# Gated-delta inverse: the last level computed as one 64-row quarter

## The reference, cut to what matters

```
kk = jnp.einsum('bhnid,bhnjd->bhnij', k, k)
lower = jnp.where(strict, beta[..., :, None] * kk * decay, 0.0)
rhs = jnp.concatenate([v * beta[..., None], k * (beta * jnp.exp(g_cum))[..., None]], axis=-1)
sol = lax.linalg.triangular_solve(lower + eye, rhs, left_side=True, lower=True, unit_diagonal=True)
```

## Time and profile before

| | us |
|---|---|
| median of three runs | 3823.49 |
| lowest, highest | 3817.28, 3826.62 |
| the profiled execution | 3812.9 |
| its span, first to last instruction | 3811.1 |
| granted TensorE clock, mean over the span | 0.97 |
| TensorE matmuls busy | 3521.2 (92%) |
| VectorE busy | 2263.3 (59%) |
| ScalarE busy | 1843.9 (48%) |
| subtractions of the inverse, line 1868 | 60.4 (88 instructions) |

### The profile page before, as it was taken

The page is one execution under the profiler, slowest core; times in us unless marked ns, Lnnn a source line. Parts: engine busy times, 40 slices in busy tenths (PEclk is TensorE's granted clock), DMA queues, the critical chain, the costliest instruction groups (busy, mean ns, idle before and its releaser), DMA issues. The chain is left out here.

```text
span 3811.1 us, 44895 instructions
## 1 busy us (share of the span) xinstructions
PE 3521.2 (92%) x18342; PEld 2970.9 (78%) x18342; DVE 2263.3 (59%) x2508; ACT 1843.9 (48%) x2354; POOL 610.4 (16%) x208
## 2 busy tenths in 40 slices
PE   7989899999899996899999899899998799999999
PEld 6879777788788875688888778787888468787887
DVE  4566569675666667666667555545455555545654
ACT  4454356664456552456554344444443344444443
POOL 0001149571133320142401100000000000000000
PEclk9999999999999998999999999999999899999999
DMA  5532156565376752376742145454544125454453
GB/s 221 188 133 89 45 210 248 216 250 189 116 270 236 265 199 100 145 265 241 263 160 96 57 147 188 163 188 155 188 168 160 38 89 188 158 191 148 155 204 133
DMA packets 89977, 653.55 MB, mean 171 GB/s; under 512 B 10033, under 2 KB 10033, under 8 KB 10929
## 3 DMA queue, kind: packets, MB, share of 16 engines
q1 hardware_dynamic: 78768, 573.10, 41.5%
q0 software_dynamic: 11008, 77.60, 5.7%
HBM read 649.61 MB, written 1.05 MB: 171 GB/s over the span
## 5 line engine op out<-in xcount | busy, mean ns | idle before, releaser
L1562 DVE TENSOR_TENSOR w_lo<-raw,w_hi 128x2048 fp32r<-128x2048 f32 x540 | 1420.9, 2636 | 646.7 <-ACT w_hi L1080 646.4
L1080 ACT ACTIVATE w_hi<-raw 128x2048 fp32r<-128x2048 f32 x540 | 1031.2, 1913 | 592.2 <-PE acc L521 403.3
L519 PE MATMUL wrk<-w_hi,h_hi 128*128 128x512 f32 (+1 forms) x2496 | 971.2, 389 | 58.8 <-DVE w_lo L1562 37.9
L521 PE MATMUL wrk<-w_hi,h_lo 128*128 128x512 f32 (+1 forms) x2496 | 954.7, 382 | 0.0
L520 PE MATMUL wrk<-w_lo,h_hi 128*128 128x512 f32 (+1 forms) x2496 | 953.9, 382 | 0.0
L519 PEld LDWEIGHTS wrk<-w_hi,h_hi 128*128 128x128 f32 x2496 | 472.5, 189 | 155.2 <-DVE w_lo L1562 48.9
L2308 POOL TENSOR_TENSOR arena<-arena,c 128x2048 f32<-128x2048 f32 x92 | 490.7, 5342 | 472.6 <-ACT arena L1080 447.6
L521 PEld LDWEIGHTS wrk<-w_hi,h_lo 128*128 128x128 f32 x2496 | 472.2, 189 | 92.5
L520 PEld LDWEIGHTS wrk<-w_lo,h_hi 128*128 128x128 f32 x2496 | 472.8, 189 | 85.0 <-issue 0.2
L519 PE MATMUL acc<-w_hi,hid_hi 128*128 128x512 f32 x1144 | 447.4, 391 | 9.4 <-DVE hid_lo L1645 9.4
L521 PE MATMUL acc<-w_hi,hid_lo 128*128 128x512 f32 x1144 | 445.4, 389 | 0.0
(11 more groups left out here) (263 smaller groups left out, 3864.5 us busy)
## 6 DMA issues: line engine op xcount, KB each, us to landing
raw<-in_wts SPq DMA_DIRECT2D x540, 1024.0 KB, 4.8
arena<-in_mods POOLq DMA_DIRECT2D x72, 1024.0 KB, 5.2
const<-in_const SPq DMA_DIRECT2D x1, 2176.0 KB, 10.1
c<-in_bias POOLq DMA_DIRECT2D x8, 256.0 KB, 3.4
x<-in_x SPq DMA_DIRECT2D x1, 1024.0 KB, 5.3
c<-in_c SPq DMA_DIRECT2D x1, 1024.0 KB, 4.8
out<-x SPq DMA_DIRECT2D x1, 1024.0 KB, 3.9
row<-in_rows SPq DMA_DIRECT2D x1, 512.0 KB, 11.3
```

The lines of the kernel that those rows point to most:

```text
L519: nc.tensor.matmul(o, l_h, r_h, start=first, stop=False, skip_group_check=True)
L521: return nc.tensor.matmul(o, l_l, r_h, start=False, stop=last, skip_group_check=True)
L1080: return nc.scalar.activation(o, i, f, **kw)
L1562: tt(w_lo[:, ns % SLOTS, :], raw[:, ns % SLOTS, :], w_hi[:, ns % SLOTS, :].bitcast(F32), ALU.subtract).then_inc(lo_ready, 1)
```

## The change

At the last level the two blocks to be joined are the rows 0 to 63 and 64 to 127. The masked matrix has entries only in rows 0 to 63 and columns 64 to 127. The changed kernel multiplies at that level only 64 rows by 64 columns with 64 moving columns for X and YT, puts the four results side by side in 256 columns of 64 partitions of the bank, copies only that quarter and subtracts only that quarter from `g_u`. X lies on partitions 64 to 127, YT on partitions 0 to 63. Levels 0 to 4, all waits and the order of instructions are as before.

```diff
 # TensorE, X
-                                m = mm(o[:, b * P:(b + 1) * P], g_lts[:, lv % 2, 4 * a + b, :], g_vi[:, 4 * a + b, :], start=True, stop=True)
+                                if lv < nl - 1:
+                                    m = mm(o[:, b * P:(b + 1) * P], g_lts[:, lv % 2, 4 * a + b, :], g_vi[:, 4 * a + b, :], start=True, stop=True)
+                                else:
+                                    m = mm(o[64:P, b * 64:(b + 1) * 64], g_lts[0:64, lv % 2, 4 * a + b, 64:P], g_vi[0:64, 4 * a + b, 0:64], start=True, stop=True)
...
 # TensorE, YT
+                                        if lv < nl - 1:
+                                            m = mm(o[:, b * P:(b + 1) * P], lh[:, 4 * a + b, :], rh[:, 4 * a + b, :], start=True, stop=True)
+                                        else:
+                                            m = mm(o[0:64, b * 64:(b + 1) * 64], lh[64:P, 4 * a + b, 0:64], rh[64:P, 4 * a + b, 64:P], start=True, stop=True)
...
 # ScalarE
+                            if lv < len(LEVELS) - 1:
+                                copy_out(f"X{half}{lv}{grp}", g_xs[:, 4 * a:4 * a + 4, :])
+                            else:
+                                label = f"X{half}{lv}{grp}"
+                                full(label)
+                                frees(use[name, label])
+                                fn(g_xs[64:P, 4 * a:4 * a + 4, 0:64], bk(label)[64:P, 0:256].rearrange("p (a b) -> p a b", b=64), ACT.Copy).then_inc(taken, 1)
...
 # VectorE
-                                    v = flat(t[:, 4 * a:4 * a + 4, :])
-                                    tt(v, v, bk(l_), ALU.subtract).then_inc(taken, 1)
+                                    if lv < len(LEVELS) - 1:
+                                        v = flat(t[:, 4 * a:4 * a + 4, :])
+                                        tt(v, v, bk(l_), ALU.subtract).then_inc(taken, 1)
+                                    else:
+                                        v = t[0:64, 4 * a:4 * a + 4, 64:P]
+                                        tt(v, v, bk(l_)[0:64, 0:256].rearrange("p (a b) -> p a b", b=64), ALU.subtract).then_inc(taken, 1)
```

More of the change, by code:

```diff
@@ L811, in invert @@
                                     for b in range(4):
-                                        m = mm(o[:, b * P:(b + 1) * P], lh[:, 4 * a + b, :], rh[:, 4 * a + b, :], start=True, stop=True)
+                                        if lv < nl - 1:
+                                            m = mm(o[:, b * P:(b + 1) * P], lh[:, 4 * a + b, :], rh[:, 4 * a + b, :], start=True, stop=True)
+                                        else:
+                                            m = mm(o[0:64, b * 64:(b + 1) * 64], lh[64:P, 4 * a + b, 0:64], rh[64:P, 4 * a + b, 64:P], start=True, stop=True)
                                     m.then_inc(filled, 1)
@@ L1302, in invert @@
                         for a, grp in enumerate("AB"):
-                            copy_out(f"X{half}{lv}{grp}", g_xs[:, 4 * a:4 * a + 4, :])
+                            if lv < len(LEVELS) - 1:
[5 more added lines that the diff above has]
+                                fn(g_xs[64:P, 4 * a:4 * a + 4, 0:64], bk(label)[64:P, 0:256].rearrange("p (a b) -> p a b", b=64), ACT.Copy).then_inc(taken, 1)
                         jobs(lv)
```

## The result

The kernel after takes 3825.54 us (median of 21 runs, 3814.65 to 3833.16), the kernel before 3817.28 on the same chip (21 runs, 3812.01 to 3826.62). The ratio is 1.0021 with a 95% interval of [1.0013, 1.0028]: slower by 0.2%, some 8 us. Forecast was a gain of 2.8 us. The time lies inside the range, but the sign is wrong, and the interval lies wholly above 1. That it lies inside is luck in part: the forecast started from 3823.5, the median of three runs, and 21 runs of the same kernel have 3817.28.

The account below looks back on a forecast made before the run. VectorE was taken to bound the last inverse level, by `w_lo` and then two subtractions. Shorter subtractions save 0.69 us at each of four places, 2.8 in all: 3823.5 - 2.8 = 3820.7 us, range 3813 to 3830.

Parts of the forecast that it names:

- TensorE's spacing: Last inverse level: 64x64 records of X and YT stand 0.07 us apart instead of 0.112, the last alone lasting 0.24.
- the two paths: To a full YT B at the last level: by ScalarE's copy 354.23 us, by PE's own order 354.14.
- rival 2: Last level: each narrow record waits for its own weight load, spacing 0.20 us; +6.4 us, 3829.9; chance 0.03.
- 10.6 above that: The three shown runs' median, 3823.5 us, compared with 3810.1, the profile's forecast after 2.8 us less.
- The switch of shape: Array shape switches in X A and before u0: 0.15 us each, covered by `w_lo` or idle PE, costing nothing.
- ScalarE and VectorE: Last level: copies from 0.60 to about 0.39 us, worth nothing alone; subtractions from 687 to 421 ns, the deciding term.
- within 0.01: Sign of being right: the last level's first subtraction starts within 0.01 us of the end of `w_lo`.
- the sum's 1.00: `w_lo` end to u0: 0.42 + 0.11 + 0.42 + 0.05 us, a gain of 0.69 per place.
- Rival 1: Thin last level halves TensorE's clock for 6.8 us, costing 3.4 per fall; 3824 to 3834 us; chance 0.25.
- by busy time alone it is fuller than either stretch: Argument against Rival 1: last level busy 2.9 of 4.1 us, earlier stretches 1.93 and 1.92 of 3.40.
- Does it reach the end?: From u0 on PE has no gap, so work hanging on it moves forward: 2.8 us, ends 0.4 and 3.8.
- Rival 3: Behind the places, waits not hanging on PE or clock falls elsewhere take back the 2.8 us: 3823.5; chance 0.12.

Follow-up runs that it names:

- e10: The kernel after, unchanged, in a second series with a second profile: 3830.18 us, ratio 1.0021 to the kernel before.
- filled kernel: The kernel after with one unread 128x512 matmul in PE's pause before u0 at all four places; two series, 3824.13 and 3825.98 us.
- e14: The kernel before with u0 computed twice, 0.89 us more dense PE work per place: 3833.69 us, ratio 1.0043.
- e1: The kernel after with a VectorE pause (reduction over 700 constants) before the last level's first subtraction: 3828.66 us, ratio 1.0022.
- e2: The kernel after with all 128 rows used for X and YT, still 64 moving columns, copy on 128 partitions: 3823.87 us, ratio 1.0010.
- e3: The kernel before with a VectorE pause putting u0 2.6 us later per place (reduction over 2580 constants): 3841.18 us, ratio 1.0057.
- e5: The kernel before with u0 computed four times, 2.67 us later per place by dense work: 3839.92 us, ratio 1.0037.
- e6: The kernel after with u0 computed twice, 0.89 us more PE work per place: 3824.12 us, ratio 1.0003.
- e9: The kernel after with one unread 128x512 matmul in PE's pause before u0 at all four places: 3824.13 us, ratio 1.0006.
- e15: The same kernel as e9, unchanged, run again on another chip: 3825.98 us, ratio 1.0023.
- e4: The kernel before with a VectorE pause putting u0 about 1.7 us later per place (reduction over 1700 constants): 3827.05 us, ratio 1.0017.
- e7: The kernel before with unread 128x512 matmuls put into TensorE's pauses of 3.4 to 7 us: 3816.63 us, ratio 0.9982.
- e12: The same kernel as e7, unchanged, run again on another chip: 3815.25 us, ratio 0.9983.
- e13: The filled kernel with u0 computed twice, 0.89 us more PE work per place: 3819.59 us, ratio 1.0001.

## Why the prediction was wrong

**TensorE's spacing and the two paths: right.** Three figures are off without effect: 2.01 less 0.28 over 15 is a spacing of 0.115 before the change, not 0.112; half of 0.112, which rival 2 uses, is 0.056 and not 0.053; and "10.6 above that" counts from the profiled 3812.9, not from 3810.1. Records of 64x64 stand 0.06 apart where I took 0.07 (seven of line 807 in 0.59, less the 0.22 of the last, over 6), and the last alone lasts 0.22 where I took 0.24. X B resumes 0.24 after `w_lo`'s start, as the 0.23 said; YT B is full at 353.64, before `w_lo` ends. The switch of shape cost nothing that is seen.

**ScalarE and VectorE: right.** Copies 0.38 (0.39 forecast), subtractions 0.41 (0.42). The first starts at 353.83, 0.07 before the end of `w_lo` in the records where "within 0.01" was put, and the gap between the two is 0.10. So `w_lo`'s end to u0 is 0.90 on the average of the places, not the sum's 1.00 (1.01 in the list of signs): 0.80 per place, 3.2 in all, a little more than the 0.69 and 2.8.

**Rival 2 (loads not hidden): wrong, as thought.** The loads of line 807 last 134 ns each and there is one per record, yet records are 0.06 apart; so they overlap matmuls of their own row group. The Trainium skill, page "TensorE: Matmul & The Clock Gate", section Part 3, The mechanism, says they do so only across row groups; the measurement decides against that here as it did at line 1051. The same section names loads into a background weight buffer as a second case; that would fit, and no run here tells whether it is that.

**Rival 1 (the clock falls at the thinned level): real, and given too little.** I put 0.25 on it, and its price per fall, 6.8 us at half clock or 3.4, was about right: e10's two falls are just so long and cost 6.1 us together. It decides one part of the loss: 6.0 of the 8 us between e10 and the kernel before on one chip. How large that part is on average is open: the kernel after's other series, 3825.54, lies between the filled kernel's two, 3824.13 and 3825.98, and its profile had no fall at the places. The argument against it, "by busy time alone it is fuller than either stretch", is the one that failed; the earlier trace rows had already shown a stretch behind which the clock fell, with as much busy time on 40 rows as another had on 128 rows, behind which it did not.

**"Does it reach the end?": the step that failed.** The prediction had "everything that hangs on PE moves forward", with a gain that arrives whole and nothing put down for the clock behind the places. It does move (1.5 us early at 501.6), and then meets the clock otherwise at pauses hundreds of us later: by 1400 us the kernel after is 3.6 us late, at the end 12.6 in the two profiles and 8 in the medians. Rival 3 named this, "falls of the clock that come at other places than now", but with two errors: I let it take back only the 2.8 us, with 3823.5 as its end, where e14 shows 13 us on top of its own work for a shift of 0.89 us per place; and I read the spread of the runs shown as mere noise, where much of it belongs to the clock. A straight line through the 109 runs of the kernel before stands at 3824.5 us for a clock of 0.964 (3823.8 to 3825.0 if each chip is taken alone) and falls by 1.8 us for each 0.001 that the clock is higher. Some of its executions get 0.968 or more, which none of e1, e2, e3, e5, e6, e9, e14, e15 and the kernel after got (e4, with its pause of 1.7 us, did in 4 of 11). At equal clock the local gain can be seen: the line gives 3828.1 for 0.962, the median clock of the kernel after and of e15, which take 3825.54 and 3825.98. That is an estimate from the line.

**What is shown and what not.** Shown: the kernel after loses by TensorE's granted clock, away from the places for the most part; half-clock stretches also begin at the narrow level, and with full rows or a filler they do not; on one chip most of the remaining loss goes when the work behind the places is put back in time by dense work, and a larger one comes in the untouched kernel when that work is moved. Not shown: why the timing of the kernel before is a good one, and which distance between which pauses matters. The mean clock does not carry all of e14's loss either: at its 0.964 the line gives 3824.5, with its own work 3828.1, and it took 3833.69. e5, 2.67 us late per place, lost only 3.4 us beyond its work (interval -1 to +8), where e14 lost 13. Part of that is the yardstick: on e5's chip the kernel before reached 0.968 in 3 of 27 runs and took 3824.80, on e14's in 12 of 21 and took 3816.83. By their own times, less the added work, e5 and e14 stand at 3829.2 and 3830.1, and the loss hardly depends on the shift. That is a comparison across chips, so argued and not shown. The same yardstick explains most of why e9 and e15, one kernel, stand at 1.0006 and 1.0023: their own times are 1.9 us apart, and the runs of the kernel before on the two chips 5.1 the other way, with 8 of 34 and 12 of 21 at 0.968 or more. The Trainium skill, same page, Part 1, states that the monitor behind the clock runs freely and is not reset when a kernel starts. The traces agree in so far as the first half-clock stretch begins at 220.50 us in one profile of the kernel after and at 223.68 in the other. With that alone shifts of all that follows should average out over many runs, and here, over 5 to 21 runs, they did not. No run here explains it.

**A faster kernel.** The narrow change does not pay in any form that was run. The kernel before with matmuls in its long pauses (e7, e12) beats both: 0.9982 [0.9973, 0.9991] and 0.9983 [0.9974, 0.9992] on two chips.

## What to carry to other kernels

In a kernel where PE is over 90% busy but has pauses of a few us, a local gain of under 1 us per place can be smaller than what a shift of everything behind it does through the granted clock. Before believing a gain or a loss of 0.2%, look at the granted clock of every timed run, in the kernel before too: a median can move by 8 us because more or fewer of its executions get the higher clock. And follow one and the same instruction through both traces to see where time is lost. Making matmuls narrower beside a wait takes work away from the clock as well as from the array: if the time is idle anyway, leave the full shape or put a full matmul that nobody reads into the pause. Here that took the falls at the place away and still left the kernel no faster than before (e2, e9, e15). To test a shift, delay by dense work on PE, not by a pause, since the pause brings falls of its own (three of four places in e1 and e3, two in e4).

## What was unexpected in the hardware

- 128 matmul records were cut to a quarter and 3.2 us saved on the path, and the program lost 8 us; giving 3.6 us of useless matmuls back to the filled form made it 6.4 us faster (3825.98 to 3819.59).
- A level that is busy 2.66 of 3.40 us on 64x64 was followed by 6.80 us at clock 0.50, one busy 1.92 of 3.40 on full rows was not the earlier trace rows.
- One profile of each kernel would have misled: the two of the kernel after differ in whether the clock falls at the places at all.
- A shift by +0.89 and one by -0.80 us per place gave nearly the same clock in the same late stretches (0.85, and 0.83 against 0.80), in one profile each, where the kernel before and e13 have 0.93 and 0.90.
- Executions of the untouched kernel with a mean clock of 0.968 or more and those with 0.966 or less are 7 to 9 us apart on each of four chips, and both occur on each; after shifts of under 1 us per place none of e14's 5 and e15's 11 reached 0.968.
